# Summing the last gathered expert rows of a product-key layer: VectorE, ScalarE and GpSimd instead of TensorE

## The reference

```python
def chunk(ht):                                  # 128 tokens
    ...
    top, pos = lax.top_k(cand, PEER_TOPK)
    eidx = jnp.take_along_axis(cidx, pos, axis=-1)
    g = jax.nn.softmax(top, axis=-1).astype(ht.dtype)
    u = u_tab[eidx]
    v = v_tab[eidx]
    a = jax.nn.gelu(jnp.einsum('thkd,td->thk', u, ht))
    return jnp.einsum('thk,thkd->td', g * a, v)
```

## Time and profile before

| | |
|---|---|
| median of 3 runs | 2893.5 us (2889.92 to 2903.21) |
| the profiled execution, first to last instruction | 2884.6 us |
| granted TensorE clock, mean | 0.934 |
| busy, TensorE / VectorE / ScalarE / GpSimd | 88% / 52% / 29% / 27% |
| DMA | 719 MB, 249 GB/s on average |
| the dense stage | about 1876 to 2885 us |

### The profile page before, as it was taken

One profiled execution on the slowest core, in us unless ns is written; L12 is line 12 of the kernel. 1 busy time (PEld: TensorE's weight loads), 2 busy tenths in 40 slices (PEclk: granted clock), 3 DMA queues, 4 the chain that ended last, 5 costly groups with the idle time before them and its releaser, 6 DMA issues.

```text
span 2884.6 us, 35666 instructions
## 1 busy us (share of the span) xinstructions
PE 2535.0 (88%) x14451; PEld 1940.8 (67%) x14451; DVE 1498.1 (52%) x3249; ACT 841.2 (29%) x1455; POOL 793.1 (27%) x755
## 2 busy tenths in 40 slices
PE   5997898889687878769989976789999999999998
PEld 5684544357444444448766566689999989998887
DVE  3125655645200000014543999869987878764443
ACT  2114322233100000014432237734333333333332
POOL 0002310000100000010000139745565656633342
PEclk8997999999799999988999988799999999999999
DMA  8224400014599999963114003799999999989995
GB/s 319 116 88 179 175 30 29 30 61 175 214 422 420 423 421 423 421 266 111 63 54 182 30 26 112 242 375 351 362 388 378 376 354 375 387 334 357 346 357 198
DMA packets 192104, 719.00 MB, mean 249 GB/s; under 512 B 32248, under 2 KB 69152, under 8 KB 162752
## 3 DMA queue, kind: packets, MB, share of 16 engines
q1 hardware_dynamic: 128960, 490.15, 43.7%
q0 software_dynamic: 62976, 226.52, 20.5%
HBM read 659.06 MB, written 57.16 MB: 248 GB/s over the span
## 4 chain that ended last, share of the span: by engine, by line
PE 60%; DVE 18%; DMA 13%; ACT 3%; issue 3%; POOL 2%; SPq 1%; POOLq 0%; DVEq 0%; ACTq 0%
PE psum L3286 9%; PE psum L3273 9%; DMA arena<-w 8%; PE psum L1592 5%; PE psum L426 4%; PE psum L2648 4%; PE psum L2112 4%; PE psum L3235 3%; PE psum L929 3%; DVE arena L3422 3%; DVE rounded L3371 3%; PE psum L1599 2%; DMA arena<-v_rows,arena 2%; PE psum L1201 2%; PE psum L1216 1%
## 5 line engine op out<-in xcount | busy, mean ns | idle before, releaser
L3286 PEld LDWEIGHTS psum<-rounded,rounded 128*128 128x128 f32 x3072 | 453.1, 189 | 34.6 <-issue 30.0
L3286 PE MATMUL psum<-rounded,rounded 128*128 128x320 f32 x3072 | 463.9, 311 | 10.6 <-ACT arena L3338 8.0
L3273 PEld LDWEIGHTS psum<-rounded,rounded 128*128 128x128 f32 x2880 | 426.0, 189 | 28.4 <-issue 13.9
L3273 PE MATMUL psum<-rounded,rounded 128*128 128x320 f32 x2880 | 434.8, 311 | 7.9 <-DVE rounded L3371 4.5
L3222 POOL DMA_INDIRECT arena<-u_rows,arena x192 | 279.6, 1456 | 254.9 <-DVE arena L3422 150.3
L1592 PE MATMUL psum<-arena 128*64 128x256 f32 x2048 | 261.7, 420 | 82.2 <-issue 61.6
L3312 ACT ACTIVATE rounded<-arena 128x1024 fp32r<-128x1024 f32 x248 | 256.9, 1050 | 263.0 <-PE psum L3286 187.1
L3371 DVE TENSOR_TENSOR rounded<-arena,rounded 128x1024 fp32r<-128x1024 f32 x248 | 303.1, 1222 | 18.4 <-ACT rounded L3312 18.4
L1592 PEld LDWEIGHTS psum<-arena 128*64 128x64 f32 x2048 | 183.8, 152 | 172.2 <-issue 123.7
L3222 POOL DMA_INDIRECT arena<-v_rows,arena x192 | 217.4, 1132 | 237.2 <-PE psum L3235 158.2
L1704 DVE COPY arena<-psum 128x256 f32<-128x256 f32 x32 | 13.6, 425 | 445.5 <-PE psum L1645 445.5
(11 more groups left out here) (453 smaller groups left out, 3337.4 us busy)
## 6 DMA issues: line engine op xcount, KB each, us to landing
arena<-w SPq DMA_DIRECT2D x96, 2048.0 KB, 25.8
arena<-v SPq DMA_DIRECT2D x64, 1024.0 KB
arena<-uT SPq DMA_DIRECT2D x60, 1024.0 KB
arena<-wada SPq DMA_DIRECT2D x12, 2048.0 KB
arena<-wp SPq DMA_DIRECT2D x10, 2048.0 KB
arena<-gd SPq DMA_DIRECT2D x60, 320.0 KB
gd<-arena SPq DMA_DIRECT2D x8, 2048.0 KB, 16.3
xb<-arena SPq DMA_DIRECT2D x1, 12032.0 KB, 42.1
```

The source lines that it names most:

```text
L3273: ins = pe.matmul(PS[:, b, 0:DT], w[:, x, k, :], hv[:, y, :], k == 0 and i == 0, k == 7 and i == 2)
L3286: ins = pe.matmul(PS[:, b, 0:DT], w[:, y, x, :], gg[:, z, :], x == 0 and i == 0, x == 7 and i == 2)
```

## The change

The 32 rounds for the last 128 tokens go. One partition stays one token, as in the dots, and the weighted sum of 128 v rows is made row by row from unit 172 to unit 242 (`SUMS`, 128 fetches of one row for each token):

- three of four rows: VectorE, `H2T = row * ZS[:, k] + H2T` (96 operations over 128x1024; the first is a plain product);
- every fourth row (k = 3, 7, ...): ScalarE scales it by its weight, in place (the first into `H2T2`), and GpSimd adds it to `H2T2` (31 additions over 128x1024), placed in GpSimd's queue eight fetches behind that row's own fetch.

The last fold then transposes and adds both accumulators on TensorE (16 fp32 products with the identity) after unit 245 instead of 247. Beside this, the 128 dots end at unit 169 instead of 173 (`LAST_DOTS` = 117), the 16 first rounds come every 6 units instead of 7 and their fold after unit 158 instead of 173, and the turned index, its transpose and the second weight transpose are gone. The number of fetched bytes stays as it is. The core of the diff:

```diff
@@ gather_pe / gather_dv
-            for s in range(3 if n < 3 else 0):
+            for s in range(3):
...
-            if n > 1:
+            if n == 2:
                 ins = pe.transpose(PS[:, 7, 384:512], NUMF, IDENT)
...
-                if step == TURN:
+                if step == TURN and n < 3:
                     turn(n)
...
-            if n == 3:
-                dv.tensor_copy(IDXT.bitcast(U32), PS[:, 7, 384:512]).then_inc(*G.dv("it", 3))
@@ the plan
-    AHEAD = 3
+    AHEAD, LAST_DOTS = 3, 117
...
-        DOTS.setdefault(3 + 49 * k // 64 if k < FEW else 52 + 121 * (k - FEW) // 128, []).append(k)
-    WEIGHTS = {52: 0, 173: 1}
-    ROUND = {58 + 7 * r: r for r in range(FEW_ROUNDS)}
-    ROUND.update({177 + 35 * r // 16: FEW_ROUNDS + r for r in range(32)})
-    FOLD = {173: 0, len(UNITS) - 1: 1}
+        DOTS.setdefault(3 + 49 * k // 64 if k < FEW else 52 + LAST_DOTS * (k - FEW) // 128, []).append(k)
+    WEIGHTS = {52: 0, 52 + LAST_DOTS: 1}
+    ROUND = {58 + 6 * r: r for r in range(FEW_ROUNDS)}
+    FOLD = {58 + 6 * FEW_ROUNDS + 4: 0, len(UNITS) - 3: 1}
+    SUMS = {}
+    for k in range(128):
+        SUMS.setdefault(55 + LAST_DOTS + (188 - LAST_DOTS) * k // 128, []).append(k)
+
+    def by_pool(k):
+
+        return k % 4 == 3
@@ dense_po
+        def add(k):
+            row = rows_of("sum", k, 0)[0]
+            po.wait_ge(*E.ac["scaled", k])
+            if k > 7:
+                po.wait_ge(*E.po["sum", k - 4])
+            po.tensor_tensor(H2T2, H2T2, row, ALU.add).then_inc(*E.po("sum", k))
...
+        adds = [k for k in range(128) if by_pool(k) and k > 3]
         for i, (kind, k, c) in enumerate(ROWS_IN_TURN):
+            if adds and i == ROW_NO["sum", adds[0], 0] + 8:
+                add(adds.pop(0))
...
+            elif kind == "sum":
+                src, column = A["v_rows"], IDX[:, k:k + 1]
...
+        while adds:
+            add(adds.pop(0))
@@ dense_pe
+        def fold_rest():
+            pe.wait_ge(*E.dv["fold", 0, 7])
+            pe.wait_ge(*E.dv["sum", 126])
+            pe.wait_ge(*E.po["sum", 127])
+            for k in range(8):
+                for i, part in enumerate((H2T, H2T2)):
+                    ins = pe.matmul(PS[:, 6 + k // 4, 128 * (k % 4):128 * (k % 4) + 128], part[:, 128 * k:128 * k + 128],
+                                    IDENT, i == 0, i == 1)
+            ins.then_inc(*E.pe("fold", 1))
@@ dense_ac
+            for k in SUMS.get(j, []):
+                if by_pool(k):
+                    row, there = rows_of("sum", k, 0)
+                    ac.wait_ge(*E.dv["w", 1])
+                    ac.wait_ge(*there)
+                    if k == 3:
+                        ac.wait_ge(*E.pe["fold", 0])
+                    ac.activation(H2T2 if k == 3 else row, row, ACT.Copy, scale=ZS[:, k:k + 1]).then_inc(*E.ac("scaled", k))
@@ dense_dv
+            for k in SUMS.get(j, []):
+                if not by_pool(k):
+                    row, there = rows_of("sum", k, 0)
+                    dv.wait_ge(*there)
+                    if k:
+                        dv.wait_ge(*E.dv["sum", k - 2 if by_pool(k - 1) else k - 1])
+                        dv.scalar_tensor_tensor(H2T, row, ZS[:, k:k + 1], H2T, ALU.mult, ALU.add).then_inc(*E.dv("sum", k))
+                    else:
+                        dv.wait_ge(*E.dv["w", 1])
+                        dv.tensor_scalar(H2T, row, ZS[:, 0:1], None, ALU.mult).then_inc(*E.dv("sum", 0))
```

## The result

The changed kernel takes 2922.4 us (median of 5 runs, 2921.3 to 2924.3), the kernel before 2898.8 us (median of 5, 2889.9 to 2909.9): a ratio of 1.0094 with a 95% interval of 1.0073 to 1.0115, slower by some 0.9%. The forecast was 2914. The later comparisons gave the kernel before 2893 to 2897 us; ratios are always to runs beside it, and each is given as recorded with its interval, so it is not exactly the quotient of the two medians (1.0081 here). One of the eleven executions of the kernel with the moved schedule alone took 4198 us and is left out.

The account below looks back on a forecast made before the run. TensorE bounds the kernel before, DMA close behind; VectorE bounds the changed one. Row work until 2873, plus 4.7 + 4 + 7 + 8, gives 2897; 8 for moved dots, 2905; the carried-over 8.9, 2914 us. Own range 2900 to 2930, with rivals 2874 to 2938.

Parts of the forecast that it names:

- The bound moves to VectorE: In the stretch of the sums: VectorE needs 264 us, 3.8 us a unit, above TensorE's 3.52.
- The step on which the sign hangs: Each of GpSimd's 31 additions shuts out VectorE's two-SBUF-input operations, taking 2.2 us: 68 us in all, bounds 0 and 73.
- The first rival (side by side): VectorE and GpSimd run together in the sums, the 68 us falls away, GpSimd's queue is next: 2874 us; chance 0.18.
- the second (half absorbed): In the sums, additions take 34 us, VectorE's 298 is below GpSimd's 303: 2890 us, no change; chance 0.20.
- the queue time: GpSimd's queue in the sums: four rows cost 10.2 us; side by side, 119 rows at 2.4 us are 287 us.
- VectorE's stretch: VectorE's row work while the sums run: 264 us plus 68 for GpSimd's additions, 332 us, until 2873.
- The start of the sums: VectorE begins the sums when unit 171 ends, at 2541, plus 8 us for the moved dots.
- The moved dots and rounds: Units 52 to 148 ask 396 GB/s of DMA, above 387: 8 us later, from 0 to 12.
- The tail: After VectorE's row work: split and unit 245 4.7 us, last fold 4, two units 7, then 8.
- What lies around the span: The earlier kernel's three-run median, 2893.5, lies 8.9 us above its profiled span, 2884.6; this was carried over.
- The clock: Rival: TensorE's granted clock falls to 0.7 in the sums, a unit takes 5.03 us: 2934 us; chance 0.07.

## Why the prediction was right, and where its terms were off

**The bound moves to VectorE.** Right: VectorE is busy 55 of 60 us, and TensorE waits for the subtraction.

**The step on which the sign hangs**, what an addition on GpSimd takes from VectorE. I took 2.2 us each, 68 in all; measured 62 us, 2.0 each, the same with 15 additions. My cap of 2.35 us for a single one was too low (up to 2.8), but 19 of the 31 cost 1.7 to 1.8. The kernels without additions, with memsets and with all rows on VectorE each show that without this term the change would not be slower. The first rival (side by side) fell to the same rows, and so did the second (half absorbed), which needed 34 us in place of 62. The kernel with memsets, whose GpSimd is nearly as busy, comes nearest to the first rival's price: 2873 where I had 2874, and the one that leaves the additions out 2868. But in both DMA was at 0.99, and sums waited only 3 us for rows, so that agreement does not confirm the queue time which I had computed.

**VectorE's stretch.** 332 us forecast, 335 measured (2564.6 to 2899.8). This is closer than its parts: the additions took 62 us, not 68, and the rest 273 us, not 264. Of these 9 us too little, 7 to 8 are waits of the subtraction for ScalarE's copy, which I had put into the range and not into the sum. GpSimd's queue was never the bound: in the stretch its fetches waited 25 us for buffers that VectorE's sums had still to free, and no sum waited for a row.

**The start of the sums** was the largest miss: 2541 + 8 against 2564.6, 16 us. Three things are in it. The moved dots and rounds: from the product after unit 54 to the end of unit 169 passed 460.5 us (2552.1 - 2091.6) against 447.7 in the kernel before (2533.0, four units before 2547.1, less 2085.3); less 0.9 for the fold that now lies in it, 12 us where I took 8. In the seven other traces with the moved rounds the same difference is 9 to 26 us; the mean of all eight is 19 us against that one trace, and 14 against the four with rounds every 7 units. So the term was sized too low, and my upper bound of 12 with it: I had left out the lower clock behind the waits, and had counted the lack on DMA's rate alone. The start of the stage, 6.3 us later in this profile (2091.6); the nine other kernels with the same code up to there had it between 2081.5 and 2092.2, so this is scatter. And about 5 us by my own reckoning: I let VectorE begin with the row work when unit 171 ended, but unit 172's own work must wait for unit 172.

**The tail.** 24 us forecast, 20.5 measured (2899.8 to 2920.3); the 16 fp32 products took 3.7 us, as taken.

**What lies around the span.** I carried over 8.9 us, the distance of one profiled span from a median of three runs. In the changed kernel the profiled run took 2922.4 at a span of 2920.3, so 2.1 us. The 8.9 was mostly the scatter of the kernel before, whose runs lie between 2889.9 and 2909.9. Together: +16 + 3 - 3 - 7 = +9 us against the forecast of 2914, which is the 8 us measured. The total came out closer than its terms, because the errors of the start and of the span had opposite signs; that part is luck.

**The clock.** The granted clock fell to 0.89 to 0.96 in the windows of 60 us from 2600 to 2900, with TensorE busy 47 to 50 us. The 0.89 is under the 0.9 that I had named as a sign of being wrong. It cost little, since a unit becomes dearer than VectorE's 4.75 us only below 3.52/4.75 = 0.74, and VectorE waited 1 us in all for matmuls. That rival did not come about.

**The chances.** They were added up wrongly. The rival without change (2890 us) had 0.20 and the faster one (2874 us) 0.18, so "same" should have had 0.08 + 0.20 = 0.28 and "faster" 0.18.

## What to carry to other kernels

Before moving elementwise work from VectorE to GpSimd, count how much of what VectorE does beside it reads two operands from SBUF: here each addition of 2.4 us took 2.0 us from VectorE and spared it a sum of 1.2. Sharing rows with TensorE instead (a diagonal matrix as weights) cost 1.95 us a row and stretched no sum. And when one engine of three near-full ones is relieved, expect less than its relief: look at DMA's share first. Last, moving fetches closer together is not free either: here the waits that followed also brought stretches at the lower clock.

## What the runs showed of the hardware that was not expected

- GpSimd's memsets (532 ns for 128x512 fp32) left VectorE's two-input operations at 1279 and 1220 ns; only GpSimd's reading additions stretched them. The Trainium skill, page "SBUF — State Buffer", section "Who interferes with whom", says that an instruction of GpSimd that only writes does not contend with a VectorE instruction that has two SBUF inputs. Here the changed kernel and the one with memsets show both halves of it.
- An operand in PSUM costs this operation nothing: 1282 ns with the accumulator in PSUM, 1280 in SBUF. I had put 6 us on it.
- A plain product with a pointer scalar took 747 ns over 1024 columns from SBUF to SBUF (L3475, one instruction), and 1282 ns in the kernel whose accumulator lies in PSUM; the form that adds to an accumulator takes 1280.
- An indirect fetch on GpSimd waits for VectorE too: issued while a VectorE operation with two SBUF inputs runs, it ended 0.81 us (median) after that operation ended, and took 1.2 to 1.7 us in the mean. Issued on an idle VectorE, or beside one that read PSUM and SBUF, it took 0.94 us.
- The Trainium skill, page "DMA: Bandwidth & Descriptors", section "Where 436 GB/s comes from", puts the HBM limit of one core at about 358 GB/s. With one core running, the trace exceeds it again: 388 GB/s over 240 us in the kernel without additions.
